# One modulation unit behind the second half of a tile, and gla_o head by head

## The reference, cut to what matters

```
s_lat = silu(c);  s_ctx = silu(c_ctx)
shift, scale, gate = split(s_lat @ w_mod[layer] + b_mod[layer], 3)
x_in = x * (1 + scale) + shift
```

```
q_e = q * exp(b);  k_e = k * exp(-b)
o_intra = where(causal, q_e @ k_e.T, 0) @ v          (inside a chunk)
s_prev[n+1] = decay[n] * s_prev[n] + d_state[n]       (64 x 128 for each head)
o = o_intra + q_e @ s_prev
```

## Time and profile before

| what | value |
|---|---|
| time, median of 3 runs | 2875.57 us (2875.34 to 2881.52) |
| the profiled execution | 2875.34 us, span 2873.4 us |
| TensorE busy, matmuls | 2716.5 us, 95% of the span |
| VectorE, GpSimd, ScalarE busy | 1739.1, 1487.4, 1207.7 us |
| chain that ended last | TensorE 77%, VectorE 12%, DMA 5% |
| granted TensorE clock, mean | 0.966 of the full clock |

### The profile page before, as it was taken

The page is one execution under the profiler, slowest core; times in us unless marked ns, Lnnn a source line. Parts: engine busy times, 40 slices in busy tenths (PEclk is TensorE's granted clock), DMA queues, the critical chain, the costliest instruction groups (busy, mean ns, idle before and its releaser), DMA issues.

```text
span 2873.4 us, 51276 instructions
## 1 busy us (share of the span) xinstructions
PE 2716.5 (95%) x22179; PEld 2515.2 (88%) x22179; DVE 1739.1 (61%) x1903; ACT 1207.7 (42%) x1438; POOL 1487.4 (52%) x1071
## 2 busy tenths in 40 slices
PE   5799999999999999999999969899999898999999
PEld 3489899888888999889989959899989798999999
DVE  2344554655555658686677656964776658745753
ACT  1233444433433434344576354532453445434452
POOL 0056766976666787665436826534548755400000
PEclk8699999999999999999999979999999999999999
DMA  9999998998887988776546837755658776644465
GB/s 339 282 313 265 268 267 246 297 274 255 244 234 229 292 249 225 202 209 182 156 140 188 231 87 209 205 147 150 166 160 219 198 189 185 162 113 115 127 168 154
DMA packets 948768, 599.21 MB, mean 209 GB/s; under 512 B 22070, under 2 KB 945088, under 8 KB 948032
## 3 DMA queue, kind: packets, MB, share of 16 engines
q1 hardware_dynamic: 944720, 582.83, 72.6%
q10 hardware_dynamic: 3824, 13.11, 1.2%
HBM read 589.46 MB, written 6.29 MB: 207 GB/s over the span
## 4 chain that ended last, share of the span: by engine, by line
PE 77%; DVE 12%; DMA 5%; ACT 3%; issue 2%; SPq 1%; ACTq 0%; DVEq 0%
PE G L2385 57%; DVE ring_r L1461 3%; DMA ring<-in_w_mod_dram 2%; PE A L2325 2%; DMA const<-in_w_mod_dram 2%; DVE S L2216 1%; PE A L2445 1%; PE A L2451 1%; PE A L2448 1%; PE G L2467 1%; PE A L2486 1%; ACT ring_r L862 1%; PE A L2630 1%; PE G L2823 1%; PE A L2835 1%
## 5 line engine op out<-in xcount | busy, mean ns | idle before, releaser
L2385 PE MATMUL G<-H_r,ring_r 128*128 128x256 f32 x10032 | 1704.3, 287 | 58.8 <-DVE S_r L1450 21.9
L2385 PEld LDWEIGHTS G<-H_r,ring_r 128*128 128x128 f32 x10032 | 1476.0, 192 | 92.4 <-issue 61.9
L819 POOL TENSOR_TENSOR ring<-ring,act_in 128x512 f32<-128x512 f32 x448 | 665.7, 1506 | 959.7 <-DMA ring<-in_w_ada_dram 717.9
L1461 DVE TENSOR_TENSOR ring_r<-ring,ring_r 128x2048 fp32r<-128x2048 f32 x346 | 860.1, 2487 | 279.1 <-ACT ring_r L862 278.1
L862 ACT ACTIVATE ring_r<-ring 128x2048 fp32r<-128x2048 f32 x346 | 661.7, 1912 | 315.6 <-PE G L2385 99.2
L2385 PE MATMUL G<-M_r,ring_r 128*128 128x256 f32 x4528 | 789.6, 284 | 0.0
L2385 PEld LDWEIGHTS G<-M_r,ring_r 128*128 128x128 f32 x4528 | 645.5, 190 | 10.0 <-issue 9.4
L2385 PE MATMUL G<-S_r,ring_r 128*128 128x256 f32 x1920 | 549.6, 286 | 0.0
L822 POOL TENSOR_TENSOR ring<-ring 128x512 f32<-128x512 f32 x224 | 369.7, 1650 | 17.6
L2385 PEld LDWEIGHTS G<-S_r,ring_r 128*128 128x128 f32 x1920 | 372.9, 194 | 3.4 <-issue 3.3
L828 POOL TENSOR_TENSOR ring<-ring 128x256 f32<-128x256 f32 x168 | 204.2, 1216 | 13.2
(11 more groups left out here) (440 smaller groups left out, 2604.8 us busy)
## 6 DMA issues: line engine op xcount, KB each, us to landing
ring<-in_w_in_dram SPq DMA_DIRECT2D x120, 1024.0 KB, 5.7
ring<-in_a_w_in_dram SPq DMA_DIRECT2D x98, 1024.0 KB, 6.8
ring<-in_w_ada_dram SPq DMA_DIRECT2D x192, 512.0 KB, 6.8
const<-in_w_mod_dram SPq DMA_DIRECT2D x192, 256.0 KB, 5.3
ring<-in_c_w_in_dram SPq DMA_DIRECT2D x48, 1024.0 KB, 5.8
ring<-in_w_mod_dram SPq DMA_DIRECT2D x16, 2048.0 KB, 18.1
ring<-in_a_w_out_dram SPq DMA_DIRECT2D x32, 1024.0 KB, 6.4
ring<-in_w_out_dram SPq DMA_DIRECT2D x32, 1024.0 KB, 5.9
```

Source lines behind the costliest of these rows:

```text
L819: g.mark(pool.tensor_tensor(w[:, i:i + 2, :], w[:, i:i + 2, :], act_in[:, k:k + 2, c:c + 1].broadcast_to((P, 2, BW)), ALU.mult))
L1461: v.tensor_tensor(w_low(tl), w_raw(tl), w_up(tl).bitcast(F32), ALU.subtract).then_inc(w_lo, 1)
L2385: ins = pe.matmul(G[tl.bank][:, 0:SEQ], w, x, start=(k == 0 and n_ == 0), stop=(k == KT - 1 and n_ == 2))
```

## The change

Two places of TensorE's program are changed. In tiles with three units the third one is issued behind the second half of the tile, ahead of the step of slot 2j + 1, and no longer behind the first two. In gla_o the loops are turned around: each head does all its chunks before the next head starts, where before the two heads of a pair took turns. The matmuls, their operands and their number stay the same, and so do the programs of all other engines.

```diff
-                gemv_units(GEMV_AT.get(q, ()))
+                gemv_units(GEMV_AT.get(q, [])[0:2])
...
                         if half == 0:
                             after_first_half(q)
+                        else:
+                            gemv_units(GEMV_AT.get(q, [])[2:])
                         if chain is not None:
                             chain.upto(2 * j + half)
...
-                    for p in range(2):
-                        for t in range(2):
-                            for b in range(2):
-                                h = 2 * p + b
+                    for h in range(GLA_H):
+                        p, b, o = h // 2, h % 2, 64 * (h % 2)
+                        for c in range(NCH):
+                            t = c // 2
+                            if c % 2 == 0:
                                 pe.matmul(G[2 + b][:, p * SEQ + t * P:p * SEQ + (t + 1) * P], GV[:, t, h * P:(h + 1) * P],
                                           gla["att"][:, b, (2 * p + t) * P:(2 * p + t + 1) * P], start=True, stop=False,
                                           skip_group_check=True)
-                            for c in range(max(1, 2 * t), 2 * t + 2):
-                                for b in range(2):
-                                    o = 64 * b
-                                    ins = pe.matmul(G[2 + b][:, p * SEQ + c * CHUNK:p * SEQ + (c + 1) * CHUNK],
-                                                    gla["st"][o:o + 64, c - 1, p * P:(p + 1) * P],
-                                                    qe[o:o + 64, p, c * CHUNK:(c + 1) * CHUNK], start=False, stop=True,
-                                                    skip_group_check=True)
+                            if c:
+                                ins = pe.matmul(G[2 + b][:, p * SEQ + c * CHUNK:p * SEQ + (c + 1) * CHUNK],
+                                                gla["st"][o:o + 64, c - 1, p * P:(p + 1) * P],
+                                                qe[o:o + 64, p, c * CHUNK:(c + 1) * CHUNK], start=False, stop=True,
+                                                skip_group_check=True)
```

## The result

The changed kernel takes 2893.9 us (median of 8 runs, 2884.96 to 2896.65), the kernel before 2875.65 in the 8 runs beside it: ratio 1.0056, 95% interval 1.0045 to 1.0068. By the ratio that is +16 us (13 to 20), by the two medians +18, where +9 was forecast: slower as forecast, but the median is 4.9 us over the upper end of the range. The profiled execution, at 2885.66 us, is one of the fastest of the changed kernel; 1 us off the forecast, it alone would seem to confirm it.

A forecast was written before the change was run, and what follows sets the result against it. TensorE, with 77% of the chain, was taken to bound the kernel. The moved units (+3.8 us) and gla_o's order (+5.4 us) summed to +9.2 us, giving 2884.7 us, with a range of 2879 to 2889 us.

The forecast's parts named there:

- The lone burst: One unit alone at L2325: 0.57 us plus 0.20 in the main matmuls behind it, 0.77 us in all.
- a split: Third unit moved out of its burst where TensorE is full: +0.35 us each, bounds 0 to 0.43.
- the units together: All sixteen moved third units: twelve splits at +4.2 us, tile 9 at -0.4, the others 0; +3.8 us.
- tile 8: At the start, where weights are late: gains 0.74 us, pays 0.77 for the lone unit, taken as 0.
- tile 9: At the start, where weights are late: gains 1.16 us, pays 0.77 for the lone unit, -0.4 us.
- gla_o's order: gla_o head by head: 7.00 us a layer instead of 4.28, +2.7 a layer, +5.4 us in both.
- SyncE was held: Rival: weights or units come late behind each pair, notably around tile 53, by 1.8 us; 2886.5 us, chance 0.10.
- swallow the cost: Rival: waits at 605.83 and behind both gla_o take in the added time; 2877.7 us, not slower, chance 0.12.
- The one of 4.09 us at 605.83: TensorE's wait after the saturated stretch; the swallowing rival had it take in six splits and tile 9, 1.7 us.
- the chance of slower: Stated as 0.75: forecast, clock and SyncE cases together, less part of the forecast's low end.
- a rival with a chance of 0.18: Granted clock falls in gla_o's thin work: 1.2 us for each layer hit, 2885.9 to 2887.1 us, chance 0.18.
- the fall behind 1990.91: After mixed 64- and 128-row work, clock 0.64 over 24 main matmuls, 4.13 us for the usual 2.92.

The follow-up runs named there:

- With the clock kept up: Both parts of the change, but gla_o's heads 2 and 3 behind the second half of the tile, against the kernel before: ratio 1.0031, +8.9 us.
- the two kernels that cut it: gla_o head by head with 24 main matmuls between heads 1 and 2, against the kernel before: 1.0013 with units as before, 1.0031 with units moved.

## Why the prediction was wrong

Right were the sums at full clock. The lone burst (0.77 forecast) is 0.56 + 0.20 in the chain, a split 0.34 for 0.35, the units together +4.6 measured for +3.8. At tile 8 the burst got 0.76 us shorter for a forecast 0.74, at tile 9 0.74 for 1.16. The prediction had put the whole 2.48 us of tile 9's burst to late weights, but part of it was the clock, 0.82 in that stretch; in the changed kernel the burst ran at 0.53, so the two do not compare as they stand. gla_o's order costs 2.7 us a layer, head by head as worked out: 0.42, 0.36, 0.42, 0.59. With the clock kept up the whole change costs +8.9 for +9.2. SyncE was held by nothing that shows: in the profiled execution no lone unit waited for its weights, and the burst behind tile 53 waited 0.90 us for 0.92. The waits did not swallow the cost. The one of 4.09 us at 605.83 is 4.21 in the changed kernel, at 608.41. What the profiled execution got back there, 2.4 us up to the burst near 632, came with the clock: 23.89 us at 0.93 against 26.27 at 0.82. Another 3.2 us came back between the two gla_o; from where, no run isolates. A slip without weight: the parts of the chance of slower add up to 0.73 at most, not 0.75.

Wrong was the step that priced gla_o "at the full clock" and left the clock to a rival with a chance of 0.18 and 1.2 us a layer. That rival is what happened, in every trace of gla_o head by head in one piece, and a fall costs 2.9 us and more a layer. Two mistakes are in it. The price came from the fall behind 1990.91, where only the 24 main matmuls behind the thin stretch were counted; here 6.8 us lie at the lower level, and they cover the end of gla_o as well as most of a tile. And the chance was weighed on two stretches of under 4 us, one with a fall behind it and one without, for a stretch of 7 us.

That the range missed follows from the same step: with 2 x 2.9 us for the clock the sum is 9.2 + 5.8 = 15.0, or 2890.7 us, inside the measured interval (13 to 20 us more than before) and outside the stated range.

What stays open is where the border lies. The clock fell at 7.0 us head by head (6 of 6). It did not fall at 3.5 us head by head (8 of 8 pieces, in the two kernels that cut it) or at 8.9 us of paired heads (2 of 2). But it fell at chunk 1 of the delta rule, a mixed stretch of only 3.9 us, in 17 of 20 places, and at chunk 2, with the same matmuls in 3.7 us, in 1 of 20. So the stretch alone does not decide it, and no run shows what else does. Nor is it shown what in the new order brings the fall, the lost pairing or the 16 changes of form in 7.0 us; the old order twice over has as many changes in 8.9 us and no fall.

## What to carry to other kernels

When an order of matmuls is changed, count three things besides the instructions: how many groups of rows or columns work side by side, how often the form changes (0.14 to 0.17 us each time here), and whether a long stretch of such thin work forms. The last can cost as much again in the granted clock (2.9 us beside 2.7 here), and putting dense matmuls in between avoided it here at no price that the runs show. A forecast for such a stretch should be made at both clock levels, and when one execution agrees with it, the spread of the timed runs still has to be looked at.

## What the runs showed of the hardware

The granted clock fell to the 1.2 GHz level although TensorE was busy without a gap and waited for no engine (8.55 us busy in a stretch of 8.55, at 0.79). The Trainium skill (TensorE: Matmul & The Clock Gate, HAM oscillation) ties such falls to waits for DMA between bursts. Here the clock fell in busy stretches (6 of 6), and with 24 dense matmuls between two pieces it stayed up (8 of 8).

A 32-column unit alone takes as long (0.56 us) as two side by side (0.57), and half-height records alone as long as in pairs: two in 0.36 us behind a change of form, against four in 0.37.
